# Hybrid decoder layer on one core: queries and keys projected in transposed form, the first mixer tile's branches issued inside the projection

## The chip, the cores and the metric

The kernel runs on one core of a Trainium2 chip. TensorE (PE in the rows) has two clock levels, 1.2 and 2.4 GHz; the granted clock is shown as a share of the higher one. The metric is the device time of one execution in microseconds (us). Lower is better.

## What is computed

One layer of a decoder with two parallel branches over a prompt of 2048 tokens and 8 samples of 8 new tokens (2112 tokens, 128 to a tile: 16 full tiles and one of 64 rows):

```python
xn = rmsnorm(x, g_pre);  u = xn @ w_in          # 1024 -> 10240 columns that matter here, plus 16 low-rank
gq, gk, gv, gg, glr, dq, dk, dv, dg, ga, gb = split(u)
# branch A: gated linear attention, 4 heads, chunks of 64 tokens
att = (gq*exp(b)) . (gk*exp(-b));  o_a = att @ gv + (gq*exp(b)) @ state
# branch B: causal windows 128/512/2048 with dilation 1/4/16, 4 heads of 128 each
s = dq_g . dk_g * HD**-0.5 (masked);  o_g, lse_g = softmax(s) @ dv_g
y_a = (rmsnorm(o_a)*silu(gg)) @ w_gla_branch;  y_b = (mix of o_g by lse)*silu(dg) @ w_dil_branch
h = x + rmsnorm((sigmoid(ga)*y_a + sigmoid(gb)*y_b) @ w_out, g_post)
y = h + (pe @ w_ple_proj) * sigmoid(h @ w_ple_gate)
```

The caches of keys and values, shifted by 8 rows, and the states are outputs too.

## The kernel before

**The projection.** Every product of f32 operands with weights is made of three f16 products (high by high, high by low, low by high part). `u` has 20 column tiles of 512 (`ORDER`), each with 17 token tiles. A token tile takes two **slots**, half of the contraction each: 4 pieces of 128 times 3 products, 12 matmuls with 512 moving columns. The token tile `xn_hi`/`xn_lo` is the stationary operand, the weights `w_hi`/`w_lo` move (L2285). A result is copied out of PSUM by ScalarE (ACT, even tiles) or VectorE (DVE, odd tiles) into `stage` and stored by SyncE (SP) into the DRAM scratch `U`.

**Side work.** All else is written into the same slot loop, in program order behind a slot's matmuls: `Gla` (recurrence over the prompt, 16 steps, one each 6 slots, from `GLA_SLOT`), `SampleGla`, `Windows` (attention over the prompt: 3 groups of 4 heads of 16 blocks, a block a slot, from `WINDOW_SLOTS`), `Samples` (attention of the samples, from `SAMPLE_SLOT` = 526). The slot numbers fix the order on each engine; semaphores do the rest. The loads of these parts are issued by GpSimd (POOL).

`Gla` loads queries and keys as rows (tokens in partitions), turns them with eight PE transposes a step (L569) into PSUM, from which VectorE multiplies (L660 to L676). `Windows` does the same for each block: transposes of `q` (L1025) and `k` (L1026), ScalarE copies both to SBUF, one slot later PE multiplies `qT` (stationary) with `kT` (L1033).

**The mixer.** `Mix` goes over the 17 token tiles in turns. For a tile t: `load_early`, `weigh`/`combine`/`make_z` on VectorE, `z_hi_half`/`z_lo_half` split z in two f16 rows (and the row `pe_in` of the per-layer input, `pe_row`), `turn_z` and `turn_pe` are DMA transposes on SP's queue; then on PE the branches (72 matmuls), and one turn later `out` (48), two turns later `gate` and `proj` (60). `z_hi_half` writes `pe_row` only after `turn_pe` of the tile ahead has landed. Before the change z of tile 0 is made at slots 660 (`PREPARE_SLOT`) and 666 (`TURN_SLOT`), its transposes are issued in slot 672, and all its matmuls stand behind the last slot, 679. The weights for `out`, `gate` and `proj` lie where `xn_hi` lay, so their loads wait for the last projection matmul.

**The start.** SP's order of loads is x of group 0 (4 tiles), weights `raw` 0 and 1, x of group 1, `raw` 2 and 3, x of groups 2 to 4, `raw` 4 and 5; `load_raw(i)` waits until piece i-2 is cut. VectorE scales the four tiles of a group (L274) before PE turns them (L288); for group 1 this stands behind the cut of piece 4 on VectorE.

Of the kernel before, what the change touches and what calls it, by code (L numbers as in the profile page):

```python
# [9 lines left out]
F32 = mybir.dt.float32  # L10
# [138 lines left out]
def sample_mask():  # L149

    mask = np.full((P, KEYS), MASKED, np.float32)
    for t in range(DEC_SEQ):
# [5 lines left out]
        for g, (window, dil) in enumerate(WINDOWS):  # L158
# [12 lines left out]
         + [U_GG, U_GG + BANK, U_DG, U_GA, U_GA + BANK, U_GB, U_GB + BANK])  # L171
GLA_TILES = 4
GLA_SLOT, GLA_PERIOD = GLA_TILES * TILE_SLOTS + 4, 6
GLA_SAMPLE_SLOT = 246
WINDOW_SLOTS = [274, 348, 450]
# [13 lines left out]
class Inputs:  # L189
# [80 lines left out]
    def scale(self, dve, i):  # L270
        tiles, rows = self.GROUPS[i]
        dve.wait_ge(self.rstd_ready, i + 1)
        for t in range(tiles):
            dve.tensor_scalar(self.x[i][:rows, t, :], self.x[i][:rows, t, :], self.rstd[i][:rows, t:t + 1], None, ALU.mult).then_inc(self.scaled, 1)  # L274
# [88 lines left out]
class Gla:  # L363


    def __init__(self, core, bind, bank, U, row0, C, halves, steps, period, state_in, state_out, L, w_lr, b_lr, causal, starts,
                 identity, OA, name):
        sb, sem = bind
        self.U, self.row0, self.C, self.halves, self.steps, self.period = U, row0, C, halves, steps, period
# [5 lines left out]
        self.qk = [sb(f"qk{s}", [T, 2 * GLA_KEY]) for s in range(2)]  # L375
# [23 lines left out]
        self.Q = self.ATT = bank[1]  # L399
        self.K = bank[2]  # L400
# [15 lines left out]
        self.qk_turned = one("qk_turned")  # L416
# [98 lines left out]
    def tensor(self, pe, r):  # L515
        decays, prepare, attend, finish = self.parts(r)
        T, C, halves, HT = self.T, self.C, self.halves, HEADS * self.T
# [10 lines left out]
        if attend is not None:  # L528
# [33 lines left out]
        if prepare is not None:  # L562
            c, s = prepare, prepare % 2
            pe.wait_ge(self.qk_loaded[s], 16 * (c // 2) + 16)
            wait(pe, self.scaled, c)
            wait(pe, self.state_ready, c)
            for n in range(2 * HEADS):
                h = n % HEADS
                last = pe.transpose((self.Q if n < HEADS else self.K)[:, h * T:(h + 1) * T], self.qk[s][:, n * P:(n + 1) * P], self.identity[:T, :T])  # L569
            last.then_inc(self.qk_turned, 1)  # L570
# [42 lines left out]
    def vector(self, dve, r):  # L613
        decays, prepare, attend, finish = self.parts(r)
        T, C, halves, flat, part, wide = self.T, self.C, self.halves, self.flat, self.part, self.wide
# [28 lines left out]
        if prepare is not None:  # L644
# [8 lines left out]
            dve.wait_ge(self.qk_turned, c + 1)  # L653
# [5 lines left out]
            if halves == 2:  # L659
                dve.scalar_tensor_tensor(out=self.q_late[:, :, :], in0=part(self.Q, 1), scalar=scale, in1=grow[:, :, 1, :],  # L660
                                         op0=ALU.mult, op1=ALU.mult).then_inc(self.crossing_ready, 1)
            dve.scalar_tensor_tensor(out=self.q_in[s][:, :, 0, :], in0=part(self.Q, 0), scalar=scale, in1=grow[:, :, 0, :],
                                     op0=ALU.mult, op1=ALU.mult)
            dve.wait_ge(self.end_ready, c + 1)
            dve.tensor_tensor(self.k_end[:, :, halves - 1, :], part(self.K, halves - 1), end_decay[:, :, halves - 1, :], ALU.mult)
            ends = [grow[:, :, b, C - 1:C] for b in range(halves)]
            if halves == 2:
                dve.tensor_tensor(self.k_early[:, :, :], part(self.K, 0), end_decay[:, :, 0, :], ALU.mult).then_inc(self.crossing_ready, 1)
# [1689 lines left out]
```

## Time and profile before

| | |
|---|---|
| time, median of 3 runs | 2999.48 us (2994.94 to 3001.77) |
| time of the profiled execution | 3000.38 us |
| its span | 2998.5 us |
| granted TensorE clock, mean | 0.99 |
| busy: PE / PEld / DVE / ACT / POOL | 97% / 53% / 34% / 30% / 12% |
| chain that ended last, by line | L2285 54%, L1912 (mixer products) 22% |

The span is the profiled part of that execution; the 1.9 us around it are in every run. PEld is the load of the stationary operand, which can go on beside a matmul. A matmul's duration in the rows overlaps with the next one's; what an instruction costs is read from the distance of two starts. A bracket behind a timeline row is the idle time ahead of it and what ended it.

### The profile page before, as it was taken

Reading aid. Unit: us, or ns where it says so; the run is one execution under the profiler, and the core shown is the slowest. Engines: PE = TensorE matmul, PEld = TensorE weight load, DVE = VectorE, ACT = ScalarE, POOL = GpSimd, SP = SyncE. Lnnn points to the kernel's source line nnn. Section 1 sums busy time; section 2 is a strip of 40 time slices with the busy share of each in tenths; the row PEclk is TensorE's granted clock in tenths of the full one; section 3 lists DMA queues with packets and bytes.
Section 4 is the critical chain, followed back from the end, with each engine's and each line's share of the span. In section 5 each row is a group of like instructions: output and inputs, shape, how many; then the busy total and the mean of one; then the engine's idle time right before and its main releaser. Section 6 shows DMA issues by size and latency. Waiting matters only on the chain.

```text
span 2998.5 us, 43562 instructions
## 1 busy us (share of the span) xinstructions
PE 2922.6 (97%) x17472; PEld 1575.0 (53%) x17472; DVE 1018.9 (34%) x2368; ACT 905.3 (30%) x1917; POOL 346.5 (12%) x573
## 2 busy tenths in 40 slices
PE   6999999999999999999999999999998799999998
PEld 3544456666545665566456655555553344444444
DVE  4311134444332433344123321112113455555542
ACT  4201123343322332333123322222212344444431
POOL 0000010000311012220011022221200000000000
PEclk9999999999999999999999999999999899999999
DMA  5234354544566575574567675665636666666651
GB/s 197 86 114 146 120 180 146 173 169 172 183 237 230 167 200 178 176 246 134 184 237 250 184 263 204 232 228 178 227 131 250 171 168 168 157 168 169 169 107 32
DMA packets 290672, 534.62 MB, mean 178 GB/s; under 512 B 152749, under 2 KB 157685, under 8 KB 288025
## 3 DMA queue, kind: packets, MB, share of 16 engines
q1 hardware_dynamic: 242746, 289.37, 32.0%
q0 software_dynamic: 47728, 242.49, 23.8%
q8 instruction: 140, 2.29, 0.3%
q14 instruction: 58, 0.48, 0.1%
HBM read 361.74 MB, written 236.67 MB: 200 GB/s over the span
## 4 chain that ended last, share of the span: by engine, by line
PE 94%; DMA 3%; DVE 1%; ACT 0%; SPq 0%; issue 0%; POOL 0%; POOLq 0%; ACTq 0%
PE out L2285 54%; PE out L1912 22%; PE out L1048 2%; PE out L1033 2%; PE out L2288 2%; PE out L1243 2%; PE out L1039 1%; PE out L549 1%; PE out L1257 1%; PE out L559 1%; PE out L560 1%; PE out L1277 1%; PE out L1025 1%; DMA mix_peT0l<-mix_pe_rowl 1%; PE out L1026 1%; PE out L288 1%
## 5 line engine op out<-in xcount | busy, mean ns | idle before, releaser
L2285 PE MATMUL out<-w_hi,xn_hi 128*128 128x512 f16 x2560 | 974.4, 381 | 1.7 <-DVE w_lo L2173 1.7
L2285 PE MATMUL out<-w_lo,xn_hi 128*128 128x512 f16 x2560 | 973.3, 380 | 0.0
L2285 PE MATMUL out<-w_hi,xn_lo 128*128 128x512 f16 x2560 | 973.1, 380 | 0.0
L2285 PEld LDWEIGHTS out<-w_hi,xn_lo 128*128 128x128 f16 x2560 | 251.1, 98 | 304.1 <-issue 3.5
L2285 PEld LDWEIGHTS out<-w_hi,xn_hi 128*128 128x128 f16 x2560 | 251.3, 98 | 281.1 <-issue 18.0
L2285 PEld LDWEIGHTS out<-w_lo,xn_hi 128*128 128x128 f16 x2560 | 251.1, 98 | 266.3 <-issue 2.9
L2201 ACT ACTIVATE stage<-out 128x512 f32<-128x512 f32 (+1 forms) x170 | 99.4, 584 | 878.4 <-PE out L2285 840.2
L2233 DVE TENSOR_SCALAR stage<-out 128x512 f32<-128x512 f32 (+1 forms) x170 | 114.8, 675 | 642.2 <-PE out L2285 612.4
L1078 DVE CUSTOM_DVE_ANT_0 score<-out,mask 128x128 f32<-128x128 f32 (+1 forms) x192 | 70.1, 365 | 317.0 <-PE out L1033 303.7
L1057 ACT ACTIVATE qT<-out 128x128 f32<-128x128 f32 x192 | 53.0, 276 | 352.9 <-PE out L1026 352.8
L1912 PE MATMUL out<-mix_w_hi,mix_zTh 128*128 128x512 f16 (+1 forms) x408 | 123.2, 384 | 27.8 <-DMA mix_zTl<-mix_z_rowl 27.8
L2173 DVE SCALAR_TENSOR_TENSOR w_lo<-raw,w_hi 128x1024 f16<-128x1024 f32 x80 | 97.6, 1221 | 128.8 <-ACT w_hi L2167 128.6
L2127 POOL DMA_DIRECT2D out<-in_cache_kv_w x88 | 45.8, 521 | 692.2 <-DVE w_lo L2173 691.9
L1912 PE MATMUL out<-mix_w_hi,mix_zTl 128*128 128x512 f16 (+1 forms) x408 | 122.7, 383 | 0.0
L1912 PE MATMUL out<-mix_w_lo,mix_zTh 128*128 128x512 f16 (+1 forms) x408 | 122.7, 383 | 0.0
L1289 ACT ACTIVATE sw_kT<-out 128x512 f32<-128x512 f32 x112 | 58.0, 570 | 151.5 <-PE out L1257 110.7
L1048 PE MATMUL out<-v,probT 128*128 128x128 f32 x600 | 98.3, 275 | 0.0
L1033 PE MATMUL out<-kT,qT 128*128 128x256 f32 (+1 forms) x384 | 97.5, 336 | 0.8 <-DVE top L1078 0.8
L1064 ACT ACTIVATE prob<-score,result 128x128 f32<-128x128 f32 (+1 forms) x192 | 89.3, 465 | 5.4 <-DVE result L1081 5.4
L2167 ACT ACTIVATE w_hi<-raw 128x1024 f16<-128x1024 f32 x80 | 84.0, 1052 | 9.2 <-DMA raw<-in_w_in 9.2
L1048 PEld LDWEIGHTS out<-v,probT 128*128 128x128 f32 x600 | 82.3, 191 | 1.4
L1912 PE MATMUL out<-mix_w_hi,mix_hTh 128*128 128x512 f16 (+1 forms) x272 | 80.9, 379 | 1.5 <-DMA mix_hTl<-mix_h_rowl 1.5
(288 smaller groups left out, 3737.6 us busy)
## 6 DMA issues: line engine op xcount, KB each, us to landing
U<-stage SPq DMA_DIRECT2D x320, 256.0 KB, 2.9
out<-in_cache_kv_w POOLq DMA_DIRECT2D x64, 1020.0 KB, 8.8
raw<-in_w_in SPq DMA_DIRECT2D x80, 512.0 KB, 4.6
sw_kc<-in_cache_kv_w POOLq DMA_DIRECT2D x24, 1024.0 KB, 6.3
sw_vc<-in_cache_kv_w POOLq DMA_DIRECT2D x24, 1024.0 KB, 9.9
out<-in_cache_kv_w POOLq DMA_DIRECT2D x16, 1008.0 KB, 7.3
mix_og<-OG SPq DMA_DIRECT2D x16, 780.0 KB, 5.1
OG<-result POOLq DMA_DIRECT2D x8, 1040.0 KB, 12.5
```

What stands on the lines that cost most here:

```text
L1033: pe.matmul(out, self.qT[n % 2][:, :], keys, start=True, stop=True).then_inc(self.scored, 1)
L1048: last = pe.matmul(self.OUT[:, :HD], self.probT[n % 2][:, i, :], self.v[h % 2][:, b - dil * (1 - i), :], start=(i == a), stop=(i == 1))
L1064: act.activation(self.prob[n % 2][:, a:, :], self.score[n % 2][:, a:, :], ACT.Exp, scale=SCALE, bias=result[:, b, HD:HD + 1], accum_out=re ...
L1078: dve.tensor_tensor_reduce(self.score[n % 2][:, a:, :], self.SCORE[:, a * P:2 * P].rearrange("p (a j) -> p a j", j=P), self.mask[:, a:, :] ...
L1243: last = pe.transpose(self.KT[n % 2][:, h * P:h * P + keys], src[:, h * P:(h + 1) * P], self.identity[:keys, :keys])
L1912: made = pe.matmul(out[n][:rows, :], a[:, k, :rows], b[:, at + k, n * BANK:(n + 1) * BANK], start=(k == 0 and i == 0), stop=(k == last and ...
L2167: act.activation(w_hi[n % 2][:, p * PIECE:(p + 1) * PIECE, :], raw[i % RAW][:, :, :], ACT.Copy, scale=W_SCALE).then_inc(hi_ready, 1)
L2173: dve.scalar_tensor_tensor(out=w_lo[n % 2][:, part, :], in0=raw[i % RAW][:, :, :], scalar=W_SCALE, in1=w_hi[n % 2][:, part, :], op0=ALU.mu ...
L2201: move_out(act, m, lambda o, x: act.activation(o, x, ACT.Copy, scale=1.0 / W_SCALE))
L2233: move_out(dve, m, lambda o, x: dve.tensor_scalar(o, x, 1.0 / W_SCALE, None, ALU.mult))
L2285: last = pe.matmul(out[m % 3][:, :], x[:, k, at:at + P], y[:, k, :], start=first, stop=final)
L2288: last = pe.matmul(out[m % 3][c * rows:(c + 1) * rows, :HALF], x[:, k, at:at + rows], y[:, k, c * HALF:(c + 1) * HALF], start=first, stop= ...
```

## The change

1. `ORDER`'s column tiles of the recurrence's queries and keys and of the attention's queries (`TURNED`, 5 of 20) are projected with the weights stationary and 512 tokens moving, so the result is already transposed. It is stored in a new scratch `UT`. The number of matmuls is the same. The 64 sample tokens are projected as before.
2. `Gla` loads its queries and keys transposed, has no transposes for them, and VectorE reads them from SBUF.
3. `Windows` loads a head's transposed queries as 128 rows of 2048 tokens. A block's queries are a strided slice of it (stride 1, 4 or 16 elements), which is the stationary operand as it stands. The transpose and the copy of `q` are gone; the keys stay as they were. `WINDOW_SLOTS` moves by 3, 3 and 2 slots.
4. At the start ScalarE scales two of the four first tiles, and `raw` 4 and 5 are loaded ahead of x of groups 2 to 4.
5. The mixer's tile 0 has its branches in slot 670, in banks that are free then; z of tile 1 is prepared at slot 672, tile 0 is merged at slot 676, and the transposes of z(1) are issued in slot 677. Behind the projection come the weights of `out`, then the transposes of m(0), then the other weights. In a turn `z_hi_half` and `make_z` of the next tile go ahead of `merge` of this one.

```diff
+TURNED = [U_GQ, U_GK] + [U_DQ + g * WIDTH for g in range(GROUPS)]
-WINDOW_SLOTS = [274, 348, 450]
+WINDOW_SLOTS = [277, 351, 452]
...
+    def scale_first(self, act):
+        act.wait_ge(self.rstd_ready, 1)
+        for t in range(self.TILES // 2, self.TILES):
+            act.activation(self.x[0][:, t, :], self.x[0][:, t, :], ACT.Copy, scale=self.rstd[0][:, t:t + 1]).then_inc(self.scaled, 1)
...
-        wait(q, self.qk_turned, c - 1)
-        q.dma_start(self.qk[s][:, :], self.U[self.rows(c), U_GQ:U_GQ + 2 * GLA_KEY]).then_inc(self.qk_loaded[s], 16)
+        wait(q, self.scaled, c - 1)
+        q.dma_start(self.qk[s][:, :, :], self.UT[T_GQ:T_GQ + 2 * GLA_KEY, self.rows(c)].rearrange("(n p) t -> p n t", p=P)).then_inc(self.qk_loaded[s], 16)
...
-            for n in range(2 * HEADS):
-                last = pe.transpose((self.Q if n < HEADS else self.K)[:, h * T:(h + 1) * T], self.qk[s][:, n * P:(n + 1) * P], self.identity[:T, :T])
...
+    def queries(self, h, b, dil):
+        at = b // dil * dil * SPAN + b % dil
+        return self.qT[h % 2][:, at:at + (SPAN - 1) * dil + 1:dil]
...
-            pe.transpose(self.TURN[:, 0:P], self.q[h % 2][:, b, :], self.identity[:, :])
-            pe.transpose(self.TURN[:, P:2 * P], self.k[h % 2][:, b, :], self.identity[:, :]).then_inc(self.turned, 1)
+            pe.transpose(self.TURN[:, 0:P], self.k[h % 2][:, b, :], self.identity[:, :]).then_inc(self.turned, 1)
...
-            pe.matmul(out, self.qT[n % 2][:, :], keys, start=True, stop=True).then_inc(self.scored, 1)
+            pe.matmul(out, self.queries(h, b, dil), keys, start=True, stop=True).then_inc(self.scored, 1)
...
-    TURN_SLOT = PREPARE_SLOT + 6
+    TURN_SLOT = PREPARE_SLOT + 4
+    PRODUCT_SLOT = TURN_SLOT + 6
+    NEXT_SLOT = PRODUCT_SLOT + 2
+    MERGE_SLOT = NEXT_SLOT + 4
...
+            self.turn_z(sp, 0)
+            self.turn_pe(sp, 0)
+            self.load_early(sp, 1)
             stores.wait_projected(sp, (COLUMN_TILES - 1) * TOKEN_TILES + 1)
             self.load_gates(sp, 0)
-        if slot == self.TURN_SLOT + 6:
-            self.turn_z(sp, 0)
-            self.load_early(sp, 1)
+        if slot == self.MERGE_SLOT + 1:
+            self.turn_z(sp, 1)
+            self.load_early(sp, 2)
...
-            for i in range(RAW, PIECES):
+            for i in range(RAW, PIECES + RAW):
                 load_raw(sp, i)
...
+                            if rows == P and ORDER[n] in TURNED:
+                                group, block = divmod(t, BANK // P)
+                                last = pe.matmul(out[m % 3][:, :], y[:, k, block * P:(block + 1) * P], x[:, k, group * BANK:(group + 1) * BANK],
+                                                 start=first, stop=final)
```

How it moves instructions on PE, in a slot of `Windows`: before (L1025 the transpose of q, L1026 that of k, L1033 the scores, L1039 and L1048 the probabilities and their product with v):

```order
L2285 MATMUL out<-w_hi,xn_lo 128x512
L1025 MATMUL out<-identity,q 128x128
L1026 MATMUL out<-identity,k 128x128
L1033 MATMUL out<-kT,qT 128x256
L1039 MATMUL out<-identity,prob 128x128 x2
L1048 MATMUL out<-v,probT 128x128 x2
L2285 MATMUL out<-w_hi,xn_hi 128x512
```

and the same place of the changed kernel (L2346 is the projection):

```order
L2346 MATMUL out<-w_hi,xn_lo 128x512
L1034 MATMUL out<-identity,k 128x128
L1043 MATMUL out<-kT,qT 128x256
L1049 MATMUL out<-identity,prob 128x128 x2
L1058 MATMUL out<-v,probT 128x128 x2
L2346 MATMUL out<-w_hi,xn_hi 128x512
```

One transpose of 128 columns is gone, nothing takes its place; `qT` is now read where the load put it.

On SP's queue behind the last stores of the projection, before (`mix_w_hi`, `mix_w_lo` 128x8192 are 2 MB each, first for `out`, then for `gate`; 128x2048 is `proj`):

```order
L2090 DMA U<-stage 64x256 x2
L1611 DMA mix_g_post_sb<-in_g_post 128x1024
L1589 DMA mix_w_hi<-CUT_HI 128x8192
L1589 DMA mix_w_lo<-CUT_LO 128x8192
L1589 DMA mix_w_hi<-CUT_HI 128x8192
L1589 DMA mix_w_lo<-CUT_LO 128x8192
L1589 DMA mix_w_hi<-CUT_HI 128x2048
L1589 DMA mix_w_lo<-CUT_LO 128x2048
L1570 DMA_TRANSPOSE mix_peT0h<-mix_pe_rowh 128x2x128
L1570 DMA_TRANSPOSE mix_peT0l<-mix_pe_rowl 128x2x128
```

and after (`mix_mT` is m of tile 0, `mix_peT1` the per-layer input of tile 1):

```order
L2142 DMA U<-stage 64x256 x2
L1605 DMA mix_w_hi<-CUT_HI 128x8192
L1605 DMA mix_w_lo<-CUT_LO 128x8192
L1593 DMA_TRANSPOSE mix_mTh<-mix_m_rowh 128x8x128
L1593 DMA_TRANSPOSE mix_mTl<-mix_m_rowl 128x8x128
L1571 DMA mix_x<-in_x_prompt 128x1024
L1638 DMA mix_g_post_sb<-in_g_post 128x1024
L1605 DMA mix_w_hi<-CUT_HI 128x8192
L1605 DMA mix_w_lo<-CUT_LO 128x8192
L1605 DMA mix_w_hi<-CUT_HI 128x2048
L1605 DMA mix_w_lo<-CUT_LO 128x2048
L1586 DMA_TRANSPOSE mix_peT1h<-mix_pe_rowh 128x2x128
```

The first `turn_pe` behind all the weights was that of tile 0; now it is that of tile 1.

At the start of SP's queue, before:

```order
L239 DMA x<-in_x_prompt 128x1024 x4
L2034 DMA raw<-in_w_in 128x2x512 x2
L239 DMA x<-in_x_prompt 128x1024 x8
L239 DMA x<-in_x_sample 64x1024
L2070 DMA glr<-in_w_in 128x8x16
L2034 DMA raw<-in_w_in 128x2x512 x2
```

and after:

```order
L241 DMA x<-in_x_prompt 128x1024 x4
L2084 DMA raw<-in_w_in 128x2x512 x4
L241 DMA x<-in_x_prompt 128x1024 x8
L241 DMA x<-in_x_sample 64x1024
L2120 DMA glr<-in_w_in 128x8x16
```

Two pieces of weights moved ahead of 4.25 MB of x.

## Rows read from the trace of the kernel before

**Rows 1.** The page: PE's busy time.
```profile
PE 2922.6 (97%) x17472; PEld 1575.0 (53%) x17472; DVE 1018.9 (34%) x2368; ACT 905.3 (30%) x1917; POOL 346.5 (12%) x573
```

**Rows 2.** Waits of PE, whole span: waiting line, releaser, us, times, longest.
```profile
PE out L1912 <- DMA mix_zTl<-mix_z_rowl: 27.8, 2, 20.8
PE out L288 <- DVE x L274: 24.3, 4, 15.4
PE out L1025 <- DMA k<-U: 6.5, 1, 6.5
```

**Rows 3.** Timeline of PE in a recurrence step: start us, us, instruction.
```profile
438.18 1.04 PE L569 MATMUL out<-identity,prompt_qk 128*128 128x128 f32 x8
439.05 0.38 PE L2285 MATMUL out<-w_hi,xn_hi 128*128 128x512 f16 x1
```

**Rows 4.** Timeline of PE in one slot of the attention.
```profile
1000.99 0.27 PE L1025 MATMUL out<-identity,q 128*128 128x128 f32 x1
1001.10 0.27 PE L1026 MATMUL out<-identity,k 128*128 128x128 f32 x1
1001.21 0.60 PE L1033 MATMUL out<-kT,qT 128*128 128x256 f32 x2
```

**Rows 5.** Groups of VectorE by form: busy us, mean ns.
```profile
L1091 DVE COPY result<-out 128x128 f32<-128x128 f32 x192 | 53.9, 281 | 5.4 <-PE out L1048 5.3
L1087 DVE COPY probT<-out 128x256 f32<-128x256 f32 x108 | 45.9, 425 | 7.2 <-PE out L1039 6.1 <-issue 1.1
...
L896 DVE COPY sample_carry<-sample_grow 128x32 f32<-128x32 f32 x1 | 0.2, 177 | 0.0
```

**Rows 6.** Timeline of PE near the start.
```profile
42.16 1.97 PE L288 MATMUL out<-identity,x 128*128 128x128 f32 x8 [8.15 <-DVE x L274]
...
48.65 1.04 PE L288 MATMUL out<-identity,x 128*128 128x128 f32 x8
```

**Rows 7.** Timeline of SP's queue, start.
```profile
18.00 4.78 SPq L239 DMA_DIRECT2D x<-in_x_prompt  x8
...
24.90 5.95 SPq L2034 DMA_DIRECT2D raw<-in_w_in  x2
```

**Rows 8.** DMA issues in 24.8 to 26 us: KB each, us to landing.
```profile
raw<-in_w_in SPq DMA_DIRECT2D x1, 512.0 KB, 12.2
```

**Rows 9.** Timeline of VectorE at the start.
```profile
39.37 2.73 DVE L274 TENSOR_SCALAR x<-x,rstd 128x1024 f32<-128x1024 f32 x4
```

**Rows 10.** Timeline of PE where the attention begins.
```profile
915.94 0.47 PE L1025 MATMUL out<-identity,q 128*128 128x128 f32 x1 [6.46 <-DMA k<-U]
...
916.43 0.63 PE L2285 MATMUL out<-w_hi,xn_hi 128*128 128x512 f16 x1
...
921.55 0.42 PE L1025 MATMUL out<-identity,q 128*128 128x128 f32 x1
```

**Rows 11.** Timeline of POOL at the same place.
```profile
903.61 1.16 POOL L981 DMA_DIRECT2D k<-U  x1
```

**Rows 12.** Timeline of VectorE where the samples' attention begins.
```profile
1777.97 0.26 DVE L1309 COPY sw_qT<-out 128x96 f32<-128x96 f32 x1 [10.12 <-DMA sw_mask<-in_sample_mask]
```

**Rows 13.** Timeline of PE there: the first scores.
```profile
1779.73 0.64 PE L1257 MATMUL out<-sw_kT,sw_qT 128*32 128x128 f32 x16
```

**Rows 14.** Timeline of PE behind the projection.
```profile
2332.47 1.04 PE L1912 MATMUL out<-mix_w_hi,mix_zTh 128*128 128x512 f16 x2 [20.79 <-DMA mix_zTl<-mix_z_rowl]
...
2366.82 1.03 PE L1912 MATMUL out<-mix_w_hi,mix_zTh 128*128 128x512 f16 x2 [6.96 <-DMA mix_zTl<-mix_z_rowl]
```

**Rows 15.** DMA issues in 2298.31 to 2299.2 us (the loads for `out`).
```profile
mix_w_lo<-CUT_LO SPq DMA_DIRECT2D x1, 2048.0 KB, 13.6
```

**Rows 16.** DMA issues in 2300.5 to 2303.5 us.
```profile
mix_peT0l<-mix_pe_rowl SPq DMA_TRANSPOSE x1, 22.0
```

**Rows 17.** DMA issues in 2282.3 to 2285.5 us (z of tile 0).
```profile
mix_zTl<-mix_z_rowl SPq DMA_TRANSPOSE x1, 4.1
```

**Rows 18.** Timeline of SP's queue behind the projection.
```profile
2303.44 7.26 SPq L1570 DMA_TRANSPOSE mix_peT0l<-mix_pe_rowl  x1
```

More of the change, by code:

```diff
@@ L960, in moves, with moved @@
         return 1 if dil == 1 else BLOCKS // dil
-    def moved(self, g, h, each):
+    def moved(self, g, h):
         heads = [(gg, hh) for gg in range(GROUPS) for hh in range(HEADS) if hh % 2 == h % 2 and (gg, hh) <= (g, h)]
-        return 16 * each * sum(self.moves(gg) for gg, _ in heads)
+        return 16 * sum(self.moves(gg) for gg, _ in heads)
     def pieces(self, dram, tile, g):
@@ L1010, in done @@
         for h in range(HEADS - 2, HEADS):
-            wait(eng, self.stored[h % 2], self.moved(GROUPS - 1, h, 1))
+            wait(eng, self.stored[h % 2], self.moved(GROUPS - 1, h))
     def at(self, g, i):
@@ L1073, in vector @@
                 before = divmod(g * HEADS + h - 2, HEADS)
-                dve.wait_ge(self.stored[h % 2], self.moved(*before, 1))
+                dve.wait_ge(self.stored[h % 2], self.moved(*before))
             dve.wait_ge(self.scored, n + 1)
@@ L1746, in scalar_before @@
             self.z_hi_half(act, 0)
+        if slot == self.NEXT_SLOT:
+            self.ask(act, 1)
+            self.open_gates(act, 0)
+            self.square_a(act, 1)
+            self.silu(act, 1)
+        if slot == self.MERGE_SLOT:
+            self.z_hi_half(act, 1)
     def scalar(self, act, t):
@@ L1914, in product, with tensor_before, branches @@
         return made
+    def tensor_before(self, pe, slot):
+        if slot == self.PRODUCT_SLOT:
+            self.branches(pe, 0)
+    def branches(self, pe, t):
+        after(pe, self.z_turned, (t + 1) * 32)
+        after(pe, self.products_gated, t)
+        self.product(pe, self.A, self.zT, "gla", self.rows(t))
+        after(pe, self.ple_gated, t - 2)
+        if t == 1:
+            for e in range(2):
+                pe.wait_ge(self.staged[e], COLUMN_TILES * TOKEN_TILES // 2)
+        dil = [part[:, GLA_VAL // P:, :] for part in self.zT]
+        self.product(pe, self.branch_bank(t), dil, "dil", self.rows(t)).then_inc(self.y_made.sem, 1)
     def tensor(self, pe, t):
@@ L1918, in tensor @@
         if self.has(t):
-            after(pe, self.z_turned, (t + 1) * 32)
-            after(pe, self.products_gated, t)
-            self.product(pe, self.A, self.zT, "gla", rows(t))
-            after(pe, self.ple_gated, t - 2)
-            if t == 0:
-                for e in range(2):
-                    pe.wait_ge(self.staged[e], COLUMN_TILES * TOKEN_TILES // 2)
-            self.product(pe, self.B, [part[:, GLA_VAL // P:, :] for part in self.zT], "dil", rows(t)).then_inc(self.y_made.sem, 1)
+            self.branches(pe, t)
         if self.has(t - 1):
@@ L2106, in _ @@
             sp.wait_ge(empty_stored, 16)
-            for t in range(mix.TURNS):
+            for t in range(1, mix.TURNS):
                 mix.queue(sp, t)
@@ L2212, in _ @@
                 mix.scalar_before(act, q)
-            for t in range(mix.TURNS):
+            mix.m_hi_half(act, 0)
+            for t in range(1, mix.TURNS):
                 mix.scalar(act, t)
@@ L2260, in _ @@
                 mix.vector_before(dve, q)
-            for t in range(mix.TURNS):
+            mix.m_lo_half(dve, 0)
+            for t in range(1, mix.TURNS):
                 mix.vector(dve, t)
@@ L2308, in _ @@
                 samples.tensor(pe, q - SAMPLE_SLOT)
-            for t in range(mix.TURNS):
+                mix.tensor_before(pe, q)
+            for t in range(1, mix.TURNS):
                 mix.tensor(pe, t)
```

142 lines of the change are left out of this document (82 added, 60 removed).

## The prediction

> **What bounds the kernel now.** First the page: PE is busy for 2922.6 of 2998.5 us [rows 1], so an edit pays in one of two ways only: PE gets less work, or one of its waits goes. Second the waits of PE over the whole span [rows 2]: the transposed z behind the projection (27.8 us in two waits), scaled x at the start (24.3 us, of which 15.4 is the first), and the keys of the attention's first head (6.5 us). Everything else is covered. Third the timelines at the places that the diff touches. There the reader is to look at the distance of two starts, which is what an instruction costs PE, and at the durations behind a long wait: a 512-column matmul shows 0.63 us there, and twelve of them take 921.55 - 916.43 = 5.12 us [rows 10]. That is the lower clock level, 1.2 GHz; at the upper one it is half, 2.56 us for twelve or 0.213 us each. So a wait of 6 us and more costs some microseconds above its length.
>
> **1. Projection turned round.** The same 24 matmuls of 512 columns for a token tile, each with its own 128 stationary columns, as before. A stored tile is 256 KB in rows of 2 KB either way. Cost 0.
>
> **2. Recurrence.** Eight transposes cost 439.05 - 438.18 = 0.87 us [rows 3]; 16 steps: **-13.9 us**. VectorE reads SBUF where it read PSUM; it is not what PE waits for. The load now has 512-byte pieces, but is issued five slots (13 us or more) ahead of its use; I take 0.
>
> **3. Attention.** A transpose of q costs 1001.10 - 1000.99 = 0.11 us [rows 4]; 192 blocks: **-21.1 us**. ScalarE's copy goes too, and it only gives slack. What the change adds is a stationary operand read with gaps: groups 1 and 2 read every 4th and every 16th f32 (16 and 64 bytes apart). No row of before shows a gapped operand on PE. The two passes of a score start 0.11 us behind the k transpose and take 0.43 us together at 256 columns (0.22 each) [rows 4], so a load of the stationary operand of up to 0.11 us is hidden behind the transpose, and the second behind 0.22 us (48 blocks of group 1) or 0.11 us (16 of group 1, all 64 of group 2). The lower bound is 0: the nearest gapped read of f32 is VectorE's copy of 32 elements 32 bytes apart, 177 ns [rows 5]. Contiguous copies of 256 and 128 elements take 425 and 281 ns, 1.12 ns an element, so 32 of them would take 281 - 96 x 1.12 = 173 ns; gaps cost nothing there. The upper bound I take from PE itself: if a gapped load takes twice as long (0.21 us), 48 blocks lose 0.11 and 80 lose 0.21, **+22 us**; at three to four times it goes on by 256 us for each microsecond of load. I take 0, since the only gapped row is nearest to it.
>
> The Trainium skill speaks against this edit: "Advanced Engine Details and Errata", section "SBUF Cachelines", says that SBUF has lines of 16 bytes, that two hits on a line are needed to hide its latency, and that a different line for each access costs. Groups 1 and 2 touch a new line with each element. The page gives no price; by the rule the +22 us or more would fall due. The VectorE row does not agree with it, but no run here has yet shown it for PE.
>
> **4. First keys.** The attention begins 3 slots (7.7 us) later in PE's program, and its k load is now the first of the head: it was issued at 903.61 behind q and landed at 915.9 [rows 10, 11], PE having waited 6.46 us. Both movements exceed the wait, so it goes, and with it the slow stretch: 5.12 - 2.56 = 2.6 us. **-9.1 us**.
>
> **5. Samples' first scores.** The last group moves by only 2 slots, but `SAMPLE_SLOT` does not move: the samples' loads, which wait for the windows' buffers, are issued 2 slots = 5.2 us later against PE's program. The mask is the last of them that is needed early: VectorE waited for it until 1777.97 and then wrote `sw_qT` by 1778.2 [rows 12]; PE used that at 1779.73 [rows 13], a slack of 1.5 us. Late next is this copy: **+3.7 us**, with PE itself queued behind it; bounds 0 (loads land sooner) and 6.
>
> **6. Start.** PE waits 8.15 us for scaled x of group 1, and then runs slowly [rows 6]. The scaling began at 39.37 [rows 9], since in VectorE's program it stands behind the cut of weight piece 4, whose load was issued at 24.90 and took 12.2 us because 4 MB of x were queued at 18.0 [rows 7, 8]. Now this load has nothing ahead of it. Its issue still waits for the cut of piece 2, at about 24. With 4 to 5 us it lands by 28.5; ScalarE and VectorE then need 1.1 + 1.2 us, the scaling 2.7: 33.8, against a PE that is through with slot 3 at 33.3 (42.16 - 8.15 = 34.0 before, 0.7 sooner by the split scaling). One us for the transposes and 2.6 for the slot: 37.5 where 48.65 stood. **-11.2 us**; -8 if the load takes 7 us.
>
> **7. Behind the projection.** Let 0 be the end of the projection. Before: branches of tile 0 until 15.5 (72 x 0.216), wait 20.8 for z(1), branches, `out`(0), wait 7.0 for z(2) [rows 14]; the branches of tile 2 start at 70.8. After, tile 0's branches lie ahead of 0, behind z(0), whose transposes are issued five slots ahead and need 4.1 us [rows 17]. z(1): its transposes stand on SP's queue behind the store of a token tile that PE ends at -2.7 and ScalarE copies by -2.1; the second is issued at -0.1 and lands at 4.0. PE waits 4, then works until 19.5. `out` needs its weights. The nine loads ahead of `peT0l` (10 MB) were issued from 2298 and landed by 2303.44 + 22.0 = 2325.4 [rows 15, 16, 18]: 0.39 MB a us. From 3 on the queue holds 2.2 MB for tile 2, 1 MB of gates, 4.2 MB of `out` weights: landed at 22, m's transposes at 25. PE waits 5 us, and ends `out`(0) at 35.4. z(2) is not ready: `z_hi_half`(2) waits for `turn_pe`(1), which now stands behind the other 6.2 MB: 41; one us on each half and 5.7 for z's transposes: 47.4. Third wait, 12 us. The old stall is cut up, not removed: the gain is 70.8 - (47.4 + 15.5) = **-7.9 us**, between 0 and -16 by how fast the DMAs are. Slow clock behind the last wait is paid before and after. Later turns have PE always busy and 39 us each; their reordering gains 0.
>
> **The sum.** 13.9 + 21.1 + 9.1 + 11.2 + 7.9 - 3.7 = 59.5 us less. The profiled execution took 3000.38 us (span 2998.5), 0.9 above the median: 2940.9, by the median 2940.0. I say 2940.5. A measurement of this kernel tells about 0.2% (6 us) from nothing.
>
> **The rivals.**
> - *Gapped loads cost about double* (+22): 2963. For it: every element of 128 blocks has its own 16 bytes. Against: the VectorE row. 23%. The Trainium skill's rule on SBUF's lines (above) points to this case or the next.
> - *Gapped loads cost 3.4 times or more* (other side): with L the load time, the loss is 256 L - 33 us, and it eats the whole 59.5 at L = 0.36 us. At four times (0.43) it is 77 us: 3018. It is decided in the attention's slots of groups 1 and 2 alone. Against it speaks the VectorE row again, more strongly. 7%.
> - *The stalls only move*: the weights piece lands late at the start (+3), or DMA behind the projection gives nothing back (+8), or the mask wait is longer and slow clock follows (+5): 2949 to 2957. For it: three new waits stand where two were, all on DMA. 15%.
> - *No effect*: the added waits would have to cost 50 us; no row has that. 2%.
> - *More gain*, 2920 to 2928: other waits shrink because the 512-byte loads of q are gone. 4%.
> - The sum as it stands, 2928 to 2949: 49%.
>
> **How the numbers follow.** The time is the likeliest case. The range goes from 2928 to 2967, so that it holds the sum, the moved stalls and the double price, 49 + 15 + some 20 of 100. Faster by over 0.2%: 0.91; within 0.2%: 0.02; slower: 0.07.
>
> **What would show it.** Right: no L569 or L1025 group, 17152 instead of 17472 PE matmuls, and scores that start 0.11 us behind the k transpose in all three groups; PE's list of waits without `k<-U`, `x` down to some 15 us, three waits behind the projection, for zT(1), `mT`/weights and zT(2). Wrong: stationary loads of the scores well above those of group 0 in groups 1 and 2, and a PE time of the score that grows with them; a wait at `sw_qT` far above 4 us; the wait for z(2) at 20 us.

## The result

The changed kernel takes **2967.5 us** (median of 4 runs, 2966.3 to 2968.6) against 2998.4 for the kernel before on the same chip: a ratio of 0.990, 95% interval 0.988 to 0.9914. So it is faster by 31 us, where the prediction said 58 less; 2967.5 lies half a microsecond above the upper end of the range, and 27 above the time forecast; it is the 27 that have to be explained. The profiled execution has a span of 2966.0 us, 32.5 below the one before.

### The profile page after: what moved, and what is told of

Its sections match the earlier page's. It is cut to its first block, busy times and chain, and to the rows that moved or that the text cites. A ratio compares the mean times of both kernels' runs of the same rounds, so it can differ in the third digit from the quotient of the medians.

```text
span 2966.0 us, 42722 instructions
## 1 busy us (share of the span) xinstructions
PE 2906.8 (98%) x17152; PEld 1562.2 (53%) x17152; DVE 1019.5 (34%) x2366; ACT 874.3 (29%) x1727; POOL 342.9 (12%) x561
## 4 chain that ended last, share of the span: by engine, by line
PE 95%; DMA 2%; SPq 1%; DVE 1%; ACT 0%; issue 0%; POOL 0%; POOLq 0%; DVEq 0%
PE out L2346 41%; PE out L1954 21%; PE out L2343 13%; PE out L1043 3%; PE out L1058 2%; PE out L2349 2%; PE out L1252 2%; PE out L1049 1%; PE out L1266 1%; PE out L561 1%; PE out L572 1%; PE out L571 1%; PE out L1286 1%; PE out L1034 1%; DMA cut_raw<-in_w_dil_branch 1%; PE out L536 1%
## 5 line engine op out<-in xcount | busy, mean ns | idle before, releaser
L2346 PE MATMUL out<-w_hi,xn_hi 128*128 128x512 f16 x1920 | 729.7, 380 | 0.0
L2346 PE MATMUL out<-w_lo,xn_hi 128*128 128x512 f16 x1920 | 729.0, 380 | 0.0
L2346 PE MATMUL out<-w_hi,xn_lo 128*128 128x512 f16 x1920 | 728.6, 380 | 0.0
L2346 PEld LDWEIGHTS out<-w_hi,xn_lo 128*128 128x128 f16 x1920 | 188.2, 98 | 227.4 <-issue 1.4
L2346 PEld LDWEIGHTS out<-w_hi,xn_hi 128*128 128x128 f16 x1920 | 188.6, 98 | 208.0 <-issue 13.1
L2346 PEld LDWEIGHTS out<-w_lo,xn_hi 128*128 128x128 f16 x1920 | 188.2, 98 | 198.1 <-issue 1.0
L2343 PE MATMUL out<-xn_hi,w_hi 128*128 128x512 f16 x640 | 242.8, 379 | 2.2 <-DVE w_lo L2227 2.1
L2343 PE MATMUL out<-xn_lo,w_hi 128*128 128x512 f16 x640 | 242.6, 379 | 0.0
L2343 PE MATMUL out<-xn_hi,w_lo 128*128 128x512 f16 x640 | 242.6, 379 | 0.0
L1954 PE MATMUL out<-mix_w_hi,mix_zTh 128*128 128x512 f16 (+1 forms) x408 | 123.0, 384 | 16.2 <-DMA mix_zTl<-mix_z_rowl 16.2
L2343 PEld LDWEIGHTS out<-xn_hi,w_hi 128*128 128x128 f16 x640 | 62.8, 98 | 74.9 <-issue 3.8
```

Of the source, the lines that this page charges most:

```text
L1954: made = pe.matmul(out[n][:rows, :], a[:, k, :rows], b[:, at + k, n * BANK:(n + 1) * BANK], start=(k == 0 and i == 0), stop=(k == last and ...
L2343: last = pe.matmul(out[m % 3][:, :], y[:, k, block * P:(block + 1) * P], x[:, k, group * BANK:(group + 1) * BANK], start=first, stop=final)
L2346: last = pe.matmul(out[m % 3][:, :], x[:, k, at:at + P], y[:, k, :], start=first, stop=final)
```

## The profile after

The page's line of busy times; PE's waits over the whole span (waiting line, releaser, us, times, longest):

```profile
PE 2906.8 (98%) x17152; PEld 1562.2 (53%) x17152; DVE 1019.5 (34%) x2366; ACT 874.3 (29%) x1727; POOL 342.9 (12%) x561
```

```profile
PE out L1954 <- DMA mix_zTl<-mix_z_rowl: 16.2, 2, 12.2
PE out L297 <- DVE x L277: 15.5, 4, 14.4
PE out L1034 <- ACT kT L1067: 4.9, 1, 4.9
PE out L1266 <- DVE sw_qT L1318: 4.8, 1, 4.8
PE out L1954 <- DMA mix_mTl<-mix_m_rowl: 3.8, 1, 3.8
PE out L2343 <- DVE w_lo L2227: 2.1, 1, 2.1
PE out L1954 <- DMA mix_hTl<-mix_h_rowl: 1.8, 1, 1.8
PE out L1043 <- DVE top L1087: 1.2, 1, 1.2
```

PE has 320 matmuls less, as forecast (17472 in [rows 1]), but its busy time fell by only 15.8 us, where the 320 transposes alone are worth 35. The waits are those forecast, and one more: 4.9 us for ScalarE's copy of the keys (`kT`), with 1.2 us for VectorE's `top` (the score's row maximum) behind it. The wait for `k<-U` of [rows 2] is gone.

Where did PE's work grow? Timelines of PE in one slot of the attention, in group 0 (keys and queries of neighbouring tokens), group 1 (every 4th) and group 2 (every 16th); start us, us, instruction:

```profile
1004.53 0.27 PE L1034 MATMUL out<-identity,k 128*128 128x128 f32 x1
1004.64 0.60 PE L1043 MATMUL out<-kT,qT 128*128 128x256 f32 x2
1005.08 0.38 PE L1049 MATMUL out<-identity,prob 128*128 128x128 f32 x2
...
1252.92 0.27 PE L1034 MATMUL out<-identity,k 128*128 128x128 f32 x1
1253.03 0.73 PE L1043 MATMUL out<-kT,qT 128*128 128x256 f32 x2
1253.60 0.38 PE L1049 MATMUL out<-identity,prob 128*128 128x128 f32 x2
...
1604.41 0.27 PE L1034 MATMUL out<-identity,k 128*128 128x128 f32 x1
1604.52 0.59 PE L1043 MATMUL out<-kT,qT 128*128 128x128 f32 x2
1604.95 0.27 PE L1049 MATMUL out<-identity,prob 128*128 128x128 f32 x1
```

The distance of two starts is what to read. All scores start 0.11 us behind the k transpose, as the prediction wants it, and yet they are not equally fast. From the score to the next transpose it is 0.44 us in group 0, about the 0.43 of [rows 4]; 0.57 in group 1; and 0.43 in group 2, where 128 columns in two passes took 0.22 before. Group 1 pays 0.13 us a block at 256 columns, and the blocks with 128 columns pay 0.21. The groups of weight loads (`LDWEIGHTS`, the load of the stationary operand) say the same (busy us, mean ns); here the changed kernel:

```profile
L1043 PEld LDWEIGHTS out<-kT,qT 128*128 128x128 f32 x384 | 87.7, 273 | 14.9 <-ACT kT L1067 1.4
```

The mean over all three groups was 192 ns before and is 273; the median is 192 ns in group 0, 329 in group 1 and 311 in group 2. With 48 blocks of group 1 at 256 columns and 80 blocks at 128 columns this is 48 x 0.13 + 80 x 0.21 = 23 us.

The new wait lies at the start of the attention. Timelines of SP's queue, ScalarE and PE there:

```profile
887.16 0.77 SPq L1384 DMA_DIRECT2D cut_raw<-in_w_dil_branch  x1
```

```profile
906.89 1.06 ACT L1401 ACTIVATE cut_hi<-cut_raw 128x1024 f16<-128x1024 f32 x1 [9.24 <-DMA cut_raw<-in_w_dil_branch]
907.85 0.26 ACT L1067 ACTIVATE kT<-out 128x128 f32<-128x128 f32 x1
```

```profile
908.16 0.33 PE L1034 MATMUL out<-identity,k 128*128 128x128 f32 x1 [4.94 <-ACT kT L1067]
909.69 1.19 PE L1043 MATMUL out<-kT,qT 128*128 128x256 f32 x2 [1.20 <-DVE top L1087]
```

A mixer weight piece, which is cut into its high and low f16 parts between the attention's steps (the cutter), was issued at 887.2 and landed 19.7 us later. ScalarE executes in order: it stood at `cut_hi` until 906.9, and the copy of the keys stood behind it. The score at 909.69 shows 1.19 us where 0.60 is usual: this is the lower clock level (1.2 GHz) behind a wait. The windows of PE show it (window, its length, PE's busy time and instructions, granted clock, DMA share, GB/s): the clock is down to 0.74 in the 10 us behind the wait, and all DMA engines are busy in the 20 us before it.

```profile
880.00:900.00 20.00, 20.00 (x98) 1.00 1.02 388
900.00:910.00 10.00, 3.86 (x18) 0.92 0.99 370
910.00:920.00 10.00, 10.00 (x41) 0.74 0.72 249
920.00:940.00 20.00, 20.00 (x115) 1.00 0.20 66
```

Where the gain is made and lost shows in the start of the last token tile (64 rows) of a column tile of the projection, in us, before and after:

| column | what lies before it | before | after | gained so far |
|---|---|---|---|---|
| 0 | start | 130.9 | 118.9 | 12.0 |
| 7 | recurrence | 898.8 | 872.8 | 26.0 |
| 10 | attention, group 0 | 1278.2 | 1237.6 | 40.6 |
| 15 | groups 1 and 2, samples' start | 1832.1 | 1805.5 | 26.6 |
| 19 | samples; tile 0's branches (15.6) are inside | 2293.2 | 2282.2 | 11.0 |
| end | mixer | 2998.5 | 2966.0 | 32.5 |

From column 10 to 15 the kernel gives 14 us back, although about 104 transposes of q (11 us) were taken out there. About 20 us of that is the gaps, 2.5 us is waiting; and since the groups begin later, three blocks of work (some 3 us) have moved in from the stretch ahead, whose gain looks larger by as much.

## The experiments

Times below are medians. All runs stand against the changed kernel's 2967.5. One thing is to be kept in mind for all of them: the wait for the keys at the attention's start, 4.9 us in the changed kernel, is not a fixed size. In the profiles of runs whose edit doesn't touch group 0 or its loads it is 2.5 (kept, rawlate), 2.9 (tail2), 3.3 (contig, slot450) and 3.4 us (tail). So up to 2.4 us of a difference against the changed kernel can come from there.

### contig: stationary operand without gaps

```diff
-        at = b // dil * dil * SPAN + b % dil
-        return self.qT[h % 2][:, at:at + (SPAN - 1) * dil + 1:dil]
+        return self.qT[h % 2][:, b * SPAN:(b + 1) * SPAN]
```

> The changed kernel, but each block's queries are 128 neighbouring columns of qT in every group, not every 4th or 16th, so the attention of groups 1 and 2 gets the wrong queries; work and loads are the same. Theory (a stationary operand read with gaps loads at half the rate): the scores of groups 1 and 2 take 0.43 and 0.22 us again instead of 0.57 and 0.44, and the kernel gets 23 us faster than the changed one, about 2944 us, ratio to before 0.982. Rival (the lost time is in waits for loads and in slots that moved): the scores change, but waits of PE eat it, and the time stays within 6 us of 2967.

Measured: 2942.6 us (2941.6 to 2943.3), ratio to before 0.9815 (0.9801 to 0.983): 24.9 us less than the changed kernel. The weight loads are back at their duration of before:

```profile
L1042 PEld LDWEIGHTS out<-kT,qT 128*128 128x128 f32 x384 | 59.1, 193 | 14.9 <-ACT kT L1066 1.4
```

What this kernel leaves out is the right choice of queries, nothing of the work. So the gaps are most of the missing gain of 27 us. Of the 24.9 us, 1.6 are a shorter wait for the keys (3.3 us here, 4.9 in the changed kernel); 23.3 are left, the 23 read from the slots.

### gaps: which distance costs

```diff
-        at = b // dil * dil * SPAN + b % dil
-        return self.qT[h % 2][:, at:at + (SPAN - 1) * dil + 1:dil]
+        at, step = b * 96, {1: 2, 4: 3, 16: 4}[dil]
+        return self.qT[h % 2][:, at:at + (SPAN - 1) * step + 1:step]
```

> The changed kernel with other gaps in qT: every 2nd f32 in group 0 (8 bytes apart), every 3rd in group 1 (12 bytes), every 4th in group 2 (16 bytes); the queries are wrong ones, work and loads are the same. If what counts is how many reads fall in one line of 16 bytes: the stationary load of group 0 stays as it was (score 0.43 us at 256 columns), group 1 lies between, group 2 costs as 64 bytes did (0.44 us at 128 columns). If any gap costs: all three are slow, 0.57 us at 256 columns in groups 0 and 1.

Measured: 2963.4 us (one run; the readings are from its trace). Timelines of PE in one slot of group 0 (elements 8 bytes apart), group 1 (12 bytes) and group 2 (16 bytes):

```profile
1000.59 0.60 PE L1043 MATMUL out<-kT,qT 128*128 128x256 f32 x2
1001.03 0.38 PE L1049 MATMUL out<-identity,prob 128*128 128x128 f32 x2
...
1250.87 0.66 PE L1043 MATMUL out<-kT,qT 128*128 128x256 f32 x2
1251.37 0.38 PE L1049 MATMUL out<-identity,prob 128*128 128x128 f32 x2
...
1600.04 0.63 PE L1043 MATMUL out<-kT,qT 128*128 128x128 f32 x2
1600.50 0.27 PE L1049 MATMUL out<-identity,prob 128*128 128x128 f32 x1
```

At 8 bytes the distance is 0.44 us, as without gaps. At 12 bytes it is 0.50 (+0.06), at 16 bytes 0.46 where 0.22 stood (+0.24); in the changed kernel 64 bytes cost +0.21 at the same 128 columns. The load itself has a median of 192 ns without gaps, 196 at 8 bytes, 261 at 12, 329 at 16 (in this run and in group 1 of the changed kernel alike) and 311 at 64. So a gap of 8 bytes is next to free; the price begins between 8 and 12 bytes and does not grow from 16 to 64. The Trainium skill ("Advanced Engine Details and Errata", section "SBUF Cachelines") says that lines of SBUF hold 16 bytes and that at least two hits on a line are needed to absorb its latency. The trace agrees in all four distances: at 8 bytes every line has two hits, at 12 bytes every third, at 16 and 64 none.

### kept: a copy that closes the gaps

ScalarE copies a block's queries into a contiguous tile, in the place where it copied the transposed queries before the change.

```diff
+            if dil > 1:
+                if b == 0:
+                    act.wait_ge(self.q_loaded[h % 2], 16 * ((g * HEADS + h) // 2 + 1))
+                act.activation(self.qB[n % 2][:, :], self.queries(h, b, dil), ACT.Copy)
             act.activation(self.kT[:, b, :], self.TURN[:, 0:P], ACT.Copy).then_inc(self.turned_kept, 1)
...
-            pe.matmul(out, self.queries(h, b, dil), keys, start=True, stop=True).then_inc(self.scored, 1)
+            queries = self.qB[n % 2][:, :] if dil > 1 else self.queries(h, b, dil)
+            pe.matmul(out, queries, keys, start=True, stop=True).then_inc(self.scored, 1)
```

> The changed kernel, with ScalarE copying the 128 queries of a block (groups 1 and 2 alone) into a small contiguous tile ahead of its copy of the keys, so that PE reads its stationary operand without gaps; the output is the reference's. Theory (the gaps cost what the run with contiguous wrong queries gave back, and ScalarE's copy lies beside the projection's matmuls): 2944, between 2941 and 2948, stationary loads of the scores back to some 193 ns. Rival (the copy of 0.3 us with gaps lengthens the chain of a block and PE waits for the keys once more): a wait at the scores of 128 times 0.1 us or more, 2950 to 2960.

Measured: 2943.0 us (2941.9 to 2943.3), ratio 0.9815 (0.9801 to 0.9828), the same as with contiguous queries. Groups of weight loads, and ScalarE's timeline in a slot of group 1:

```profile
L1045 PEld LDWEIGHTS out<-kT,qB 128*128 128x128 f32 x256 | 39.3, 193 | 9.1
```

```profile
1242.93 0.44 ACT L1072 ACTIVATE qB<-qT 128x128 f32<-128x128 f32 x1 [2.49 <-PE out L1035]
1243.27 0.26 ACT L1073 ACTIVATE kT<-out 128x128 f32<-128x128 f32 x1
```

The copy costs ScalarE 0.34 us a block and PE nothing: the scores come a slot later, and ScalarE had waited 2.5 us. The rival fell: PE's only wait for a copy of the attention is the one at its start, 2.5 us. The whole term was to be had for 128 instructions on an engine with time to spare.

### hold: the second head's keys six blocks later

```diff
-        wait(q, self.turned, (n - 1) * BLOCKS)
+        wait(q, self.turned, 6 if n == 1 else (n - 1) * BLOCKS)
```

> The changed kernel, but the loads of the attention's second head wait until six blocks of the first are turned. Theory (the cutter's 512 KB load, issued five slots ahead of ScalarE's cut, queues behind the k, q and v of two heads, so ScalarE and then PE wait): the load lands in under 13 us instead of 19.7, PE's wait of 4.9 us for kT and of 1.2 us for the top go, with 1 to 3 us of slow clock: 7 to 9 us faster than the changed kernel, about 2959 us. Rival (the first head's loads and the copies alone fill the DMAs): the wait stays above 3 us and the time within 3 us of 2967.

Measured: 2961.2 us (2959.1 to 2961.8), ratio 0.9876 (0.9862 to 0.9891): 6.3 less, where 7 to 9 were expected. Timelines of ScalarE and PE:

```profile
903.56 1.06 ACT L1401 ACTIVATE cut_hi<-cut_raw 128x1024 f16<-128x1024 f32 x1 [5.24 <-DMA cut_raw<-in_w_dil_branch]
```

```profile
904.83 0.33 PE L1034 MATMUL out<-identity,k 128*128 128x128 f32 x1 [0.94 <-ACT kT L1067]
```

With the second head's loads (3 MB from 885.4 in the changed kernel) out of its way the weight piece lands after 15.7 us, not 19.7 (under 13 was expected). PE waits 0.9 us, not 4.9; the 1.2 us for `top` stay; and the granted clock in 910 to 920 is 1.00 in place of 0.74. Those are the 4.0 us of wait and some 2.6 of clock. From column 7 to 10 this kernel needs 358.2 us and the changed one 364.8; slot450, rawlate, tail and tail2, which are the same as the changed one there, need 362.1 to 363.4. So the second head's loads cost 4 to 6.6 us. What else makes the piece late (15.7 us, where the one ahead of it took 4.3) was not taken apart; the first head's loads and the cache copies are under way at that time.

### slot450: the third window group two slots earlier

```diff
-WINDOW_SLOTS = [277, 351, 452]
+WINDOW_SLOTS = [277, 351, 450]
```

> The changed kernel with the last window group at slot 450 instead of 452. Theory (the samples' mask is late because the windows end two slots later): PE's wait of 4.8 us for sw_qT and 0.4 us for sw_kc go, 5 us faster than the changed kernel, about 2962 us. Rival (the loads before the mask are slower for another reason): the wait stays.

Measured: 2962.2 us (2962.0 to 2964.2), ratio 0.9883 (0.9867 to 0.99): 5.3 less. PE no longer waits for `sw_qT` at all; VectorE's wait for the mask is 9.9 us, about as in [rows 12]; in the changed kernel it was 16.9. So the place and the reason of step 5 are right. But the 5.3 us are a net figure, since another wait comes up with group 2 at slot 450:

```profile
1495.41 0.33 PE L1034 MATMUL out<-identity,k 128*128 128x128 f32 x1 [1.83 <-ACT kT L1067]
```

From column 10 to 15 it needs 4.9 us less than the changed kernel: 4.8 and 0.4 us of waits at the samples' start and 1.6 us of slow clock behind them (0.83 granted in 1750 to 1760, 1.00 here) go, and 1.8 us come.

### rawlate: weight pieces behind x again

```diff
-            for i in range(RAW, PIECES + RAW):
+            for i in range(RAW, PIECES):
                 load_raw(sp, i)
...
+            for i in range(PIECES, PIECES + RAW):
+                load_raw(sp, i)
```

> The changed kernel, with the loads of the next column's first weight pieces back behind those of x groups 2 to 4, as before the change; the split of the scaling stays. Theory (the start's 12 us come from the order of the loads): PE's wait at slot 4 is 7 to 8 us again with slow clock behind it, 2976 to 2980. Rival (they come from the split of the first scaling): 2967 to 2969.

Measured: 2976.9 us (2975.9 to 2978.0), ratio 0.9929 (0.9915 to 0.9942): 9.5 more than the changed kernel. Timelines of PE at the first slot that needs x group 1, in the changed kernel and in this one:

```profile
33.06 1.09 PE L297 MATMUL out<-identity,x 128*128 128x128 f32 x8 [0.36 <-DVE x L277]
```

```profile
43.54 1.97 PE L297 MATMUL out<-identity,x 128*128 128x128 f32 x8 [8.08 <-DVE x L277]
```

The 8.1 us are back, and so is the doubled duration behind them [rows 6]. The load of piece 4 takes 14.3 us here from issue to landing, 12.2 before [rows 8], and 3.8 in the changed kernel. Column 0's last tile starts at 131.3, where it stood at 130.9 before the change and at 118.9 after. So none of the 12 us is had without the new order of the loads, and the split of the scaling gives nothing by itself. What it adds to the new order, where PE begins 1.0 us sooner (14.4 for 15.4), was not tried. (Of the 12.4 us, 3 are gone by the end: 2.6 of them between column 7 and 10, where the wait for the keys is 2.5 us here and 4.9 in the changed kernel.)

### tail: transposes ahead of the last weights

```diff
+        self.turn_pe(sp, 1)
         self.turn_m(sp, 0)
         self.load_x(sp, 0)
+        self.turn_z(sp, 2)
         sp.dma_start(self.g_post_sb[:, :], self.g_post.to_broadcast([P, D_MODEL])).then_inc(self.g_loaded.sem, 16)
         for name in ("gate", "proj"):
```

The two are left out of turn 1's queue.

> The changed kernel, with tile 1's transposes of pe_in ahead of tile 0's of m, and tile 2's of z ahead of the loads of g_post, gate and proj weights. Theory (the 12.2 us wait for z(2) stands because pe's transposes landed behind 4 MB of weights, and ScalarE and VectorE cut z(2) only behind them): z(2) is issued by some 2315 where it was issued at 2330; the wait falls to 0 to 2 us, 2955 to 2959 (12 us less, less what slow clock gives). Rival (z(2) is late through its own inputs, OG, OA and U of tile 2, that stand behind): the wait stays over 8 us, 2963 to 2968. Second rival: the gate weights come late and the wait moves to the gate product.

Measured: 2962.7 us (2962.2 to 2963.9), ratio 0.9882 (0.9868 to 0.9895): only 4.8 less. PE behind the projection, in the changed kernel and in this one:

```profile
2335.44 1.04 PE L1954 MATMUL out<-mix_w_hi,mix_zTh 128*128 128x512 f16 x2 [12.20 <-DMA mix_zTl<-mix_z_rowl]
```

```profile
2344.55 1.04 PE L1957 MATMUL out<-mix_w_hi,mix_mTh 128*128 128x512 f16 x2 [4.73 <-DMA mix_mTl<-mix_m_rowl]
```

The wait for z(2) goes entirely, as the theory says (its transpose was issued at 2311.1, not 2329.9), but a wait for the second `mT` comes up 9 us later. Behind column 19 this run gains 5.5 us. The gain that I expected was too large, since I had not asked what is late next.

### tail2: the last weights behind turn 1's transposes

The same edit, with the four loads of gate and proj weights moved behind `mix.queue(sp, 1)`.

> As the run with the tail's queue order, with the gate and proj weights (4 MB) now behind the whole of turn 1's queue, the transposes of tile 1's m and tile 0's h included. Theory (the 4.7 us wait for the second mT, which took the place of the one for z(2), is there because those weights and the loads of tile 3 were ahead of it): that wait is under 1 us, 2957 to 2959. Rival (mT is late through its own inputs): still over 3 us, 2962. Second rival: the gate product now waits for its weights, some 3 to 8 us, 2961 to 2966.

Measured: 2951.3 us (2949.7 to 2954.4), ratio 0.9847 (0.9833 to 0.986): 11.3 less than tail, 16.2 less than the changed kernel, where 8.5 to 10.5 were expected. Timelines of SP's queue for the second m, in tail and here:

```profile
2329.51 9.01 SPq L1593 DMA_TRANSPOSE mix_mTh<-mix_m_rowh  x1
```

```profile
2321.06 3.78 SPq L1593 DMA_TRANSPOSE mix_mTh<-mix_m_rowh  x1
```

Windows of PE at 2320 to 2360, first the changed kernel and then tail2:

```profile
2320.00:2340.00 20.00, 7.80 (x30) 0.74 1.00 296
2340.00:2360.00 20.00, 20.00 (x94) 1.00 0.66 171
```

```profile
2320.00:2340.00 20.00, 20.00 (x94) 1.00 1.01 317
2340.00:2360.00 20.00, 20.00 (x94) 1.00 1.01 288
```

PE's waits for z and m behind the projection fall from 20.0 to 7.4 us, and in 2320 to 2340 the clock stays at 1.00 where it was 0.74. From column 19 to the end this kernel needs 669.9 us, the changed one 683.8: waits of 12.6 us were worth 13.9. The other 2.3 of the 16.2 us arise earlier, where the edit changes nothing; 1.7 of them lie between column 7 and 10, with a wait for the keys of 2.9 us in place of 4.9. Of the 11.3 us against tail, 8.4 lie behind column 19 and 2.1 at the start. No wait for the gate weights appears, so the second rival fell too.

### all and all2: the edits together

> The changed kernel with four edits together: queries of groups 1 and 2 copied to contiguous tiles by ScalarE, keys of the second head loaded six blocks later, the third window group at slot 450, and the tail's queue order. If the gains stand apart they add: 2967.5 - 24 - 6 - 5 - 10 = 2922, between 2918 and 2928. Rival (they share waits, since each edit moves PE against the DMA queues): 2930 and more.

Measured: kept + hold + slot450 + tail, 2927.1 us (2927.0 to 2931.8), ratio 0.9763 (0.975 to 0.9776). The single gains (24.5 + 6.3 + 5.3 + 4.8 = 40.9) and the measured one (40.4) agree.

> The four edits together, with this tail: the combination before gave 2927.1 with two waits for mT of 10.2 us in all. If the second wait goes as in the run beside it: 2927 - 5 = 2922, between 2919 and 2926. Rival: no change against it, 2926 to 2929.

Measured: with tail2 in place of tail, **2919.2 us** (2917.9 to 2921.7), ratio to before 0.9738 (0.9725 to 0.9752). This is 48 us below the changed kernel and 78 below the one before. The single gains add to 24.5 + 6.3 + 5.3 + 16.2 = 52.3, so 4 are shared. The wait for the keys is one term that is counted more than once: hold takes 4.0 us of it, and each of the other three has a shorter one than the changed kernel (by 2.4, 1.6 and 2.0 us) without having caused it. The account beyond that was not closed. What is left of PE's waits in all2:

```profile
PE out L297 <- DVE x L277: 15.9, 4, 14.8
PE out L1965 <- DMA mix_mTl<-mix_m_rowl: 4.5, 1, 4.5
PE out L1965 <- DMA mix_zTl<-mix_z_rowl: 4.0, 1, 4.0
```

All waits of PE in all2 come to 33 us, half of them at the start, where PE waits for the first x.

## Why the prediction was wrong

**Step 3 failed: "I take 0, since the only gapped row is nearest to it".** The transposes went as costed, but the gapped stationary loads cost 23 us by the slots and by contig (24.9, less 1.6 of another wait). The step had this price as its upper bound (+22 at double the load time), and the count of blocks and the cover behind the transpose were right. What failed is the choice between the bounds: a VectorE copy of 32 elements with gaps was taken to speak for a weight load of 128. A row of another engine does not bound this one, and even for VectorE the comparison was weak: the contiguous copies it was set against read `out`, which lies in PSUM, and the gapped one reads SBUF. The rule that the step itself quoted from the Trainium skill ("Advanced Engine Details and Errata", section "SBUF Cachelines") pointed the right way. 2940.5 + 23 = 2963.5 is the rival "about double".

**Step 4 had its own part right and missed a collision.** The wait for `k<-U` went. The step did not ask what else loads at that time. The attention's first loads and the second head's are now issued at 875 to 887, and the weight piece of 887.2 is issued among them: 4 to 6.6 us, as hold shows, a slow stretch again. In the kernel before, the same piece was issued at 922.9, 19 us behind the first keys (903.61 [rows 11]) and 9 us or more behind the second head's loads, and it landed after 10.6 us. The mechanism could have been read there, at the start of groups 1 and 2. Timeline of ScalarE in the kernel before:

```profile
1198.75 1.06 ACT L1392 ACTIVATE cut_hi<-cut_raw 128x1024 f16<-128x1024 f32 x1 [5.07 <-DMA cut_raw<-in_w_out]
...
1531.65 1.06 ACT L1392 ACTIVATE cut_hi<-cut_raw 128x1024 f16<-128x1024 f32 x1 [5.92 <-DMA cut_raw<-in_w_ple_proj]
```

This is the rival "the stalls only move", with a stall that I had not named: a DMA wait of ScalarE that holds the keys' copy behind it.

**Step 2** is right: 14.0 us from column 0 to 7 (12.0 to 26.0), 13.9 forecast.

**Step 5** is right in place and too low in size: the wait for `sw_qT` is 4.8 us where 3.7 were forecast, and with 0.4 us for `sw_kc` and 1.6 us of slow clock it is 6.8, above the bound of 6.

**Step 6** is right: 12.0 us for 11.2, by the mechanism named, as rawlate shows; the transposes that stood at 48.65 start at 36.58, forecast 37.5.

**Step 7** is right in its waits, 4.0, 3.8 and 12.2 us where 4, 5 and 12 were forecast. The gain is 5.9 for 7.9 (32.5 - 11.0 - 15.6, from the table). Most of the difference is the clock, whose cost the step took to be equal before and after: there are three waits now, where two were, and each has a slow stretch behind it, in all 5.9 us where 4.3 were lost before (share of the clock not granted times the time outside the waits, without the last 8 us). The terms named for z(2) (41, one us on each half, 5.7) add to 48.7, not 47.4; the 6.4 us that were used are what the trace has from the landing of pe's transposes to that of z's (2329.0 to 2335.4). That pe's transposes stand behind the weights and hold z(2) up is confirmed by tail and tail2.

**Not foreseen on the gain's side** is that two waits for the keys' copy go, at 1200.2 and 1533.1, behind the two pieces shown above. These groups now begin 3 and 2 slots later against the cutter: at 1495.3 ScalarE still stands at `cut_hi` for 5.1 us, but PE needs nothing of it yet; with group 2 back at slot 450 the wait is there again (slot450). The list of PE's waits of the kernel before has them, in a row that the prediction passed over:

```profile
PE out L1025 <- ACT kT L1058: 5.0, 2, 2.6
```

The sum by the traces: the transposes give 35.0 us (13.9 + 21.1). All waits of PE together fall from 68.5 to 51.6 us, 16.9 less. What slow clock costs outside the waits, counted as in step 7, falls from 13.8 to 10.3 us, 3.5 less. The gaps take 23.4. That gives 32.0 us less, against 32.5 between the two spans.

Against the forecast stand the gaps (23.4 us), the new wait for the keys with `top` and its slow clock (9.0), and 3.1 us more for the mask and 2.0 less from the mixer than expected; for it stand the two waits at the groups' starts with `top` and their slow clock (9.6) and 0.8 us at the start. Together that is 27.1 us, the distance from 59.5 to 32.5. That the time came out so near the range is luck in part: the new collision and the two that went nearly cancel.

## What to carry to other kernels

When a transpose is removed by reading an operand with gaps, look at which engine reads it and how far apart: PE's stationary f32 operand of 128 columns was next to free at 8 bytes (196 ns for 192) and took 329 ns at 16, which doubled a score of 128 moving columns. If the gaps can't be avoided, let an engine with time to spare copy the block. When a load is moved earlier, list every other load in that window and which in-order engine stands behind it. Behind a removed stall, ask at once what is late next; two orders of the queue were needed here until the second stall went too. Waits on PE can be worth more than their length, by the slow clock behind them: here 13.9 us for 12.6 behind the projection, and 6.6 for 4.0 at the attention's start. And compare two runs stretch by stretch before a whole difference is credited to the edit: a wait that the edit doesn't touch moved by 2.4 us between them.

## What the runs showed of the hardware

- Stationary f32 operand with gaps, 128 columns per load, score of 128 moving columns in two passes: 0.22 us without gaps, 0.43 at 64 bytes, 0.46 at 16. At 256 moving columns: 0.43 to 0.44 without gaps and at 8 bytes, 0.50 at 12, 0.57 at 16. With more moving columns more of the load is hidden: 16 bytes cost 0.24 us at 128 and 0.13 at 256. The load's own median: 192 ns, 196 at 8 bytes, 261 at 12, 329 at 16, 311 at 64.
- ScalarE's copy of 128 elements 16 or 64 bytes apart out of SBUF took 0.41 to 0.45 us, its contiguous copy out of PSUM 0.25 to 0.28 (both in kept). Whether the gaps or the source make this difference was not tried.
- The issue of a DMA transpose of 128x8x128 behind large loads held SP's queue for 9.01 us in tail (its data had been ready since 2317, and it was issued at 2329.5, with all DMA engines busy), where the same one took 3.78 in tail2; the first one behind the weights of `out` took 10.4 us in the changed kernel. What stands behind it on the queue is late by as much. Large loads ahead are not the whole condition: two of 128x2x128 behind the gate and proj weights took 1.3 us each in the changed kernel, while one of that size took 7.26 before [rows 18]. What decides it stays open.
